# First projection of a fused two-block transformer kernel: six column groups for the first three pairs of x, four for the others, and attention six half-steps later

## What is computed

```python
mod = jax.nn.silu(c) @ w_ada[l] + b_ada[l]
sh_a, sc_a, gt_a, sh_f, sc_f, gt_f = [m[:, None, :] for m in jnp.split(mod, 6, axis=-1)]
h = rmsnorm(x, g_pre_attn[l]) * (1.0 + sc_a) + sh_a
proj = h @ w_in[l]
qa, ka, va, qb, kb, vb = jnp.split(proj, 6, axis=-1)
...
mix = jnp.concatenate([oa.reshape(B, S, WIDTH_A), ob.reshape(B, S, WIDTH_B)], axis=-1)
x = x + gt_a * rmsnorm(mix @ w_out[l], g_post_attn[l])
```

## Time and profile before

| | |
|---|---|
| median of 3 runs | 2367.99 us |
| profiled execution | 2367.4 us, its span 2365.6 us |
| TensorE (PE) busy | 2336.8 us, 99% of the span |
| VectorE (DVE) busy | 1816.1 us, 77% |
| ScalarE (ACT) busy | 1121.3 us, 47% |
| first projection, attention and output projection | 26 to 456 us of the span |
| TensorE idle in the span (span less busy) | 28.8 us |

### The profile page before, as it was taken

How to read it: one execution, slowest core, us unless ns; L and a number is a source line. 1 busy time by engine, 2 the same in 40 slices (tenths; PEclk the granted TensorE clock), 3 DMA queues, 4 the chain that set the end, 5 groups by cost and what they waited for, 6 DMA issues and landing times.

```text
span 2365.6 us, 26344 instructions
## 1 busy us (share of the span) xinstructions
PE 2336.8 (99%) x10358; PEld 1894.7 (80%) x10358; DVE 1816.1 (77%) x2447; ACT 1121.3 (47%) x1473; POOL 14.7 (1%) x31
## 2 busy tenths in 40 slices
PE   8999999999999999999999999999999999999998
PEld 5377788788888888888878888888888888888887
DVE  6788988888888888977565577997877795555775
ACT  5455676554444434444464334444345544444453
POOL 0000000000000000000000000000000000000000
PEclk9999999999999999999999999999999999999999
DMA  9987888887788777888746555556665556655553
GB/s 402 419 294 284 307 319 336 302 323 283 283 320 303 282 279 277 316 322 330 247 142 212 201 190 196 192 195 205 203 206 204 200 202 251 204 196 191 185 194 124
DMA packets 87758, 598.48 MB, mean 253 GB/s; under 512 B 10145, under 2 KB 10209, under 8 KB 16593
## 3 DMA queue, kind: packets, MB, share of 16 engines
q1 hardware_dynamic: 85538, 588.95, 69.2%
q0 software_dynamic: 1664, 7.19, 1.0%
q10 hardware_dynamic: 432, 0.66, 0.1%
HBM read 594.62 MB, written 2.13 MB: 252 GB/s over the span
## 4 chain that ended last, share of the span: by engine, by line
PE 91%; DVE 4%; DMA 3%; ACT 1%; issue 1%; DVEq 0%; ACTq 0%
PE PS L1181 20%; PE PS L1197 19%; PE PS L1198 19%; PE PS L1206 19%; PE PS L1186 10%; DMA RAW<-in_w_mod 2%; DVE RAW L1638 2%; DMA RAW<-in_w_first 1%; DVE LO L1628 1%; PE PS L1333 1%; PE PS L1552 0%; DVE X L1719 0%; PE PS L1270 0%; PE PS L1322 0%; ACT HI L669 0%
## 5 line engine op out<-in xcount | busy, mean ns | idle before, releaser
L669 ACT ACTIVATE HI<-RAW 128x1024 fp32r<-128x1024 f32 x784 | 828.4, 1059 | 1100.6 <-PE PS L1206 686.3
L1628 DVE TENSOR_TENSOR LO<-RAW,HI 128x1024 fp32r<-128x1024 f32 x784 | 956.7, 1223 | 461.9 <-ACT HI L669 457.9
L1197 PE MATMUL PS<-HI,XH 128*128 128x512 f32 x2080 | 821.8, 395 | 2.8 <-ACT HI L669 1.8
L1198 PE MATMUL PS<-HI,XL 128*128 128x512 f32 x2080 | 810.5, 390 | 0.0
L1206 PE MATMUL PS<-LO,XH 128*128 128x512 f32 x2080 | 558.3, 389 | 1.1 <-DVE LO L1628 1.1
L1197 PEld LDWEIGHTS PS<-HI,XH 128*128 128x128 f32 x2080 | 390.5, 188 | 87.4 <-DVE XL L1900 3.0
L1206 PEld LDWEIGHTS PS<-LO,XH 128*128 128x128 f32 x2080 | 390.2, 188 | 83.4 <-DVE LO L1628 1.6
L1198 PEld LDWEIGHTS PS<-HI,XL 128*128 128x128 f32 x2080 | 390.8, 188 | 78.9
L1181 PE MATMUL PS<-HI,XH 128*128 128x512 f32 x1056 | 325.9, 390 | 1.6 <-DVE XL L1742 1.1
L1181 PE MATMUL PS<-HI,XL 128*128 128x512 f32 x1056 | 325.2, 389 | 0.0
L1186 PE MATMUL PS<-LO,XH 128*128 128x512 f32 x1056 | 283.9, 389 | 0.0
(11 more groups left out here) (263 smaller groups left out, 891.6 us busy)
## 6 DMA issues: line engine op xcount, KB each, us to landing
RAW<-in_w_second SPq DMA_DIRECT2D x208, 1024.0 KB, 4.9
RAW<-in_w_mod SPq DMA_DIRECT2D x144, 1024.0 KB, 5.4
RAW<-in_w_ffn SPq DMA_DIRECT2D x88, 1024.0 KB, 4.9
RAW<-in_w_first SPq DMA_DIRECT2D x64, 1024.0 KB, 5.9
RAW<-in_w_down SPq DMA_DIRECT2D x44, 1024.0 KB, 5.1
BIAS<-in_b_in SPq DMA_DIRECT2D x40, 256.0 KB, 5.2
R<-mod_rows POOLq DMA_DIRECT2D x3, 1024.0 KB, 9.1
X<-in_x SPq DMA_DIRECT2D x2, 1024.0 KB, 8.7
```

Of the source, the lines that this page charges most:

```text
L669: act.activation(HI[:, (it["half"] + hf) % HLS, :], whole, ACT.Copy).then_inc(s.hi_ready, 1)
L1197: pe.matmul(PS[:, bank + u, :], XH[:, 2 * n + kk, rows], hi, start=start and kk == 0, stop=False)
L1198: pe.matmul(PS[:, bank + u, :], XL[:, 2 * n + kk, rows], hi, start=False, stop=False)
L1628: dve.tensor_tensor(LO[:, slot, :], RAW[:, it["slot"], hf * 1024:(hf + 1) * 1024], HI[:, slot, :].bitcast(F32), ALU.subtract).then_inc(s.l ...
```

## The change

Pairs 0 to 2 now serve six column groups: 4, 5, 2, 3 (halves 0 to 11, pair by pair), then 0 and 1 (halves 12 to 17). All 18 are direct. Groups 4 and 5 (v of the differential attention) begin in the PSUM banks of groups 0 and 1; ScalarE copies their partial sums to SBUF (`v_save`), groups 0 and 1 take the banks over, and the other five pairs of groups 4 and 5 run as halves 38 to 47. VectorE then adds the saved part (`v_add`). Pairs 3 to 7 serve groups 0 to 3 in halves 18 to 37, all in the split form. The A loads have a table of their own (`ADA_AHEAD`: how many A loads stand ahead of W load c), the later ones stand behind W loads 22 to 63 with two more behind 53 and 55. Rotations, turns, units and the first dilated heads stand six (dilated heads two, the norm and the turns of the first eight heads three or four) halves later; the 16 units now share 28 halves, so units 0 and 1 stand at 46 and 47, units 7 and 8 at 59 and 60, all others two apart.

```diff
-DIRECT = (0, 1, 2, 3)
-
-DIRECT_PAIRS = 6
-
-ADA_BEHIND = list(range(20, 64))
+AHEAD = 3
+
+PARTED = (4, 5)
+
+ADA_AHEAD = [4, 6, 8, 10, 12, 13, 14, 17, 19, 20, 22, 23, 24, 26, 28, 29, 29, 32]
+
+ADA_BEHIND = sorted([*range(22, 64), 53, 55])
...
-UNITS_AT = 40
+UNITS_AT = [46 + 28 * e // 15 for e in range(16)]
...
 def first_half(h):
 
-    if h < 8 * EARLY:
-        n, g = divmod(h, EARLY)
-    else:
-        g, n = divmod(h, 8)
+    if h < 4 * AHEAD:
+        n, r = divmod(h, 4)
+        g = (*PARTED, 2, 3)[r]
+        return g, n, n == 0, g in PARTED and n == AHEAD - 1
+    if h < 6 * AHEAD:
+        n, g = divmod(h - 4 * AHEAD, 2)
+        return g, n, n == 0, False
+    if h < 32 + 2 * AHEAD:
+        n, g = divmod(h - 2 * AHEAD, 4)
+        return g, n, False, n == 7
+    if h < 48:
+        g, n = divmod(h - 32 - 2 * AHEAD, 8 - AHEAD)
+        return PARTED[g], n + AHEAD, n == 0, n == 8 - AHEAD - 1
+    g, n = divmod(h, 8)
     return g, n, n == 0, n == 7
...
 def is_direct(h):
...
+    return h < 6 * AHEAD
...
-ROPE_AT = [31, 33, 35, 37, 59, 67, 75, 83]
-QK_TURN_AT = [(32, 33), (34, 35), (37, 38), (39, 40), (58, 60), (66, 68), (74, 76), (82, 84)]
+ROPE_AT = [37, 39, 41, 43, 59, 67, 75, 83]
+QK_TURN_AT = [(38, 39), (40, 41), (43, 44), (45, 46), (58, 60), (66, 68), (74, 76), (82, 84)]
...
-        if h - off == (74 + 2 * i if i < 4 else 76 + 2 * i):
+        if h - off == (76 + 2 * i if i < 4 else 78 + 2 * i):
...
+            def v_save(i):
+                g = PARTED[i]
+                act.wait_ge(s.half_used, 4 * AHEAD - 3 + i)
+                at = 1024 + 512 * i
+                act.activation(VO[:, :, at:at + 512], PS[:, first_bank(g):first_bank(g) + 2, :], ACT.Copy).then_inc(s.v_saved, 1)
...
-                if 92 <= h < 96:
-                    mtb_evac(h - 92)
+                if 95 <= h < 99:
+                    mtb_evac(h - 95)
...
-                if 88 <= h < 92:
-                    mixb_turn(h - 88)
+                if 91 <= h < 95:
+                    mixb_turn(h - 91)
...
+            def v_add(i):
+                g = PARTED[i]
+                dve.wait_ge(s.half_used, first_group_used(g))
+                dve.wait_ge(s.v_saved, i + 1)
+                v = VO[:, :, 1024 + 512 * i:1536 + 512 * i]
+                dve.tensor_tensor(v, PS[:, first_bank(g):first_bank(g) + 2, :], v, ALU.add).then_inc(s.v_added, 1)
...
+                if h == 46:
+                    v_add(0)
+                if h == 51:
+                    v_add(1)
```

More of the change, by code:

```diff
@@ L307, in first_body @@
 def first_body():
[L309 to L319, removed]
+    body = []
+    for c, n in enumerate(ADA_AHEAD):
+        body += [("A",)] * (n - body.count(("A",)))
+        body.append(("W", c))
+    for c in range(len(ADA_AHEAD), 64):
         body.append(("W", c))
@@ L904, in beside_first @@
                     qk_evac(*part)
-                if (i := v_at(h)) is not None:
+                if 4 * AHEAD <= h < 4 * AHEAD + 2:
+                    v_save(h - 4 * AHEAD)
+                if (i := v_at(h)) is not None and i >= 2:
                     v_evac(i)
@@ L958, in _ @@
                     hi_half(sec, 0, FIRST_W[0], 1)
-                if h < 8 * EARLY and h % EARLY == 0:
-                    x_pair(h // EARLY)
+                if (n := first_pair_at(h)) is not None:
+                    x_pair(n)
                 if 2 <= h < sec.n_halves:
@@ L1435, in _ @@
                     bank = first_bank(g)
-                    if start and g >= EARLY:
-                        before = g - 4 if g < 6 else g - 2
-                        if before in QK_GROUPS:
-                            pe.wait_ge(s.qk_out, QK_GROUPS.index(before) + 1)
-                        else:
-                            pe.wait_ge(s.v_out, V_GROUPS.index(before) + 1)
-                    if start and g == 5:
-                        pe.wait_ge(s.qt_ready, 6)
-                    if g == 0:
-                        pe.wait_ge(s.xh_ready if n < DIRECT_PAIRS else s.x_ready, n + 1)
-                    if h == 8 * EARLY:
-                        pe.wait_ge(s.x_ready, 8)
+                    if 4 * AHEAD <= h < 4 * AHEAD + 2:
+                        pe.wait_ge(s.v_saved, g + 1)
+                    if start and h >= 6 * AHEAD:
+                        held = g - 4 if g < 6 else g - 2
+                        if held in QK_GROUPS:
+                            pe.wait_ge(s.qk_out, QK_GROUPS.index(held) + 1)
+                        else:
+                            pe.wait_ge(s.v_added, V_GROUPS.index(held) + 1)
+                        if g == 5:
+                            pe.wait_ge(s.qt_ready, 4)
+                    if (pair := first_pair_at(h)) is not None:
+                        pe.wait_ge(s.xh_ready if is_direct(h) else s.x_ready, pair + 1)
                 else:
@@ L2100, in _ @@
                     h = it["half"] + hf
-                    if h < EARLY * DIRECT_PAIRS and h % EARLY == 0 and h:
-                        x_low(h // EARLY - 1)
-                    if h == EARLY * DIRECT_PAIRS:
-                        x_low(DIRECT_PAIRS - 1)
-                    if EARLY * DIRECT_PAIRS <= h < 8 * EARLY and h % EARLY == 0:
-                        x_low(h // EARLY)
+                    if h % 4 == 0 and 0 < h <= 4 * AHEAD:
+                        x_low(h // 4 - 1)
+                    if h >= 6 * AHEAD and (n := first_pair_at(h)) is not None:
+                        x_low(n)
                     if 96 <= h < 100:
@@ L2454, in first @@
     def first():
-        for n in range(16):
+        for n in range(48):
             yield [np.concatenate([rows(w["w_in"][:, W_IN_COLS[g]:W_IN_COLS[g] + 512], 2 * k, 2)
                                    for g, k, *_ in (first_half(2 * n), first_half(2 * n + 1))], axis=1)]
-        for n in range(16, 48):
-            g, k, _, _ = first_half(2 * n)
-            yield [rows(w["w_in"][:, W_IN_COLS[g]:W_IN_COLS[g] + 512], 2 * k, 4)]
         for g, k in W_OUT_CHUNKS:
```

55 lines of the change are left out of this document (29 added, 26 removed).

## The result

The changed kernel takes **2372.14 us**, the median of 13 executions (2368.28 to 2374.61); the kernel before took 2367.89 us on the same chip (13 executions). The ratio is 1.002, with a 95% interval of 1.0013 to 1.0028: slower by 0.2%. Forecast were 2364.0 us and a range from 2358 to 2370. The profiled execution took 2370.79 us, its span 2369.0 against 2365.6 us, so 3.4 of the 4.3 us between the medians are to be found in these two profiles.

The account below looks back on a forecast made before the run. TensorE, 99% busy, was taken as the bound, with loads setting the early pace. Terms 8.0 - 1.4 + 0.9 - 1.5 - 0.2 - 1.4 - 0.4 gave 4.0 us gain: profiled 2363.4, median 2364.0 us, range 2358 to 2370.

Parts of the forecast that it names:

- The start, +8.0: Up to pair 7: six more halves ahead of it, last reduction at 133.8, pair 7 at 139.5; gain 8.0 us.
- I take the second, so nothing is lost: Load buffers in the start: issue to landing takes 4.9 us as in the second block, not 7.6; cost nothing.
- The estimate of 4.4 us by the Trainium skill: Load time in the start: about 2.0 us plus bytes at 436 GB/s, by which the buffers suffice.
- `v_save`, costed at nothing: Two ScalarE copies of about 1 us, needed by TensorE three halves (10.7 us) later; cost nothing.
- The sine table was counted as a wait of VectorE, 1.8 us: Start: ScalarE's table load holds a load's second conversion back 1.8 us, most of VectorE's 2.6 us of waits.
- The rival in which the buffers run dry: Start: loads need 7.6 us from issue, pair 7 comes 8 us later, time about 2372; chance 0.08.
- The clock, -1.4: Behind the 4.0 us wait ahead of pair 7 TensorE runs at half speed; loss 1.4 us, 0 if idle comes in pieces.
- The first score and the later places, +0.9 - 1.5 - 0.2 - 1.4 - 0.4 = -2.6: Attention: lambda-table turn wait gone +0.9; unit 1's score -1.5; units 7 and 8 -0.2; half 74 turn -1.4; half 94 turn -0.4.
- The moved A loads, "meet a VectorE that is some 9 us ahead: nothing": Late in the section: two A loads moved behind W loads 53 and 55 meet VectorE some 9 us ahead; cost nothing.
- The announced signs: No TensorE waits 42 to 135 us; about 4 us near 139, then half speed; score waits 1 to 3, half 74 near 2.
- those named for a wrong forecast: Reductions waiting for loads 105 to 133 us, no second-score wait, TensorE waiting for VectorE at many units, halves waiting for `LO`.

Follow-up runs that it names:

- the tables alone: Changed kernel with only the sine and cosine tables moved from half 22 to half 19; 2369.61 us, ratio to the kernel before 1.0013.
- all three edits: Changed kernel with W load 4 one load later, both `v_save` behind the second conversion, tables at half 19 instead of 22; 2370.72 us, ratio 1.0007.
- e9_free_a_48_50: Changed kernel with all three edits, and the two later A loads behind W loads 48 and 50 instead of 53 and 55; 2366.63 us, ratio 0.9989.
- the run with zeros alone: Changed kernel with only four products of zeros added in TensorE's wait ahead of pair 7; 2371.20 us, ratio to the kernel before 1.0015.
- e12_a_48_50: Changed kernel with only the two later A loads behind W loads 48 and 50 instead of 53 and 55; 2369.59 us, ratio 1.0012.
- e1_start_free: Changed kernel with all three edits and nothing else; 2370.72 us, ratio to the kernel before 1.0007.
- e6_free_a_back: Changed kernel with all three edits, and the later A loads as before the change, one behind each W load from 20; 2367.72 us, ratio 1.0000.

## Why the prediction was wrong

**The start, +8.0: measured 4.3.** Part of the mechanism is as forecast: pair 7 follows the reductions of VectorE, back to back at the end, and the six halves ahead of it gain time. But the last reduction starts at 137.54, not at 133.8. The step that failed is the one on the buffers, "I take the second, so nothing is lost". Loads that were issued late took 6.7 to 7.8 us to land (loads 20, 24, 33, 38, 40), not the 4.9 of the second block; the lower bound was nearest to a stage with room, and this one is full. The estimate of 4.4 us by the Trainium skill (DMA: Bandwidth & Descriptors, Anatomy of one DMA) does not hold for these loads either: it rests on a fit for loads that GpSimd issues, and the shortest load of this section took 4.7 us. Two holders of a buffer were also missed: `x_pair(2)` ahead of the copies of W load 4, and `v_save`, costed at nothing because TensorE needs it late, though a load waits for the copy behind it. The sine table was counted as a wait of VectorE, 1.8 us, but as the holder of a buffer it was priced at nothing by the same 4.9. The runs with the tables alone and with all three edits show it: pair 7 moves with load 38, by 2.6 and 2.3 us. How much of this an execution keeps varies, as the profile of `e9_free_a_48_50` shows. The rival in which the buffers run dry had the right cause at the wrong size (8 us; 5.0 were lost). That its time, 2372, is what was measured is chance: the other half of that time comes from the end.

**The clock, -1.4: 1.3 by the run with zeros alone,** 1.6 with the slow first products of pair 7. Right for this profile; in the others without zeros the clock behind this wait cost 0.1 to 2.9 us. (The row of 42 to 44 us that the forecast reads lies ahead of 44.14; the window from 44 to 46 us has 1.00 as well.)

**The first score and the later places, +0.9 - 1.5 - 0.2 - 1.4 - 0.4 = -2.6: measured 2.8** from half 36 to half 97. The sum came out by chance; its parts did not. The turn's wait did not go (0.93 us at 181.52: its read-out stands behind a conversion whose load comes late), the second score waits 0.59 instead of 1.5, units 7 and 8 wait for nothing, turn and score behind the gate columns wait 1.16 us together against 0.54 before, and the turn at half 94 waits 0.66. Less the waits of the kernel before, these make 2.0 of the 2.8; the rest stands in no single wait.

**The moved A loads, "meet a VectorE that is some 9 us ahead: nothing": measured 5.7 us, of which 1.6 comes back.** In the sum of the two profiles this is the term that turned the sign; in the runs the change without it (`e12_a_48_50`) is still slower, by 0.12% instead of 0.20%, and only with the start mended too is it faster. The lead was there, 11.3 us at W load 53. But W loads 53 and 55 are now followed by two A loads each, three loads or 7.4 us for two halves of 5.4 us, and the lead falls to 7.0 us at W load 54 and 2.9 at 56. That is some 4 us each time, twice what this count gives: VectorE, whose reductions free the buffers, has more to do there as well. From 395 to 410 us it is busy 14.8 of 15 us (13.5 in the kernel before), and the share of the DMA engines is 0.93 to 1.00; which of the two sets the pace no run separates. From there to the end two halves take 5.4 us and their two loads 5.0, so the lead is hardly rebuilt (2.4 us at W load 62), and conversion and split of the last loads need more than that. I asked whether there was a lead and not what it must still cover. The run of the kernel before with this line alone (+4.3 us in the profile, 1.0031 in the runs) and that of the change with the two loads at 48 and 50 (-3.4 us) show it from both sides.

With the measured terms the sum is 4.3 - 1.6 - 2.8 - 5.7 + 1.6 + 0.7 = -3.5 us, against 3.4 us found. The announced signs came true in part: the wait ahead of pair 7 is there (3.2 us at 143 instead of 4 at 139), with the reductions ahead of it back to back and half speed behind it. But TensorE does wait between 42 and 135 us (2.75 us at 115.73). Of those named for a wrong forecast, a half that waits for `LO` came (1.77 us at 452.81). Reductions that wait for their loads between 105 and 133 us did not, although loads are late there: the conversions ahead of the splits wait for them.

## What to carry to other kernels

A load that the DMA engines work through without pause needs its buffer early: look for what stands between landing and the freeing instruction on each engine that must pass (another job's turn in the queue, a table load, an evacuation), and take the time from issue to landing from a stage that is equally full. A step that is moved into a stretch with a lead uses up that lead for everything up to the next point at which the lead is rebuilt; compare it with the least lead behind it, not with that at the place. Three small edits and a better place for two loads made the change faster than what it replaced, by 0.11% (0.02 to 0.20%, in one series).

## What the runs showed of the hardware that was not expected

The same wait costs different amounts of clock. Behind an idle time of 3.2 to 3.7 us ahead of pair 7, halves 34 and 35 took 7.04 us in the changed kernel, 8.38 and 8.32 in `e1_start_free` and `e9_free_a_48_50`, and 5.53 in `e6_free_a_back`, where the granted clock stayed at 2.4 GHz. Executions of one kernel lie 4 to 10 us apart here, those of the kernel before too (2365.6 to 2373.6 in one series of 27); the clock is part of that, how much was not measured. A profile of one execution therefore shows where a wait is, and only the series what it costs.

The time from issue to landing is not one number even in a full stage: load 30 of the changed kernel was issued at 84.08, landed at 89.39, 5.3 us later, and on time; load 38 took 6.7 us. The lead at issue does not settle it either: load 30 was issued 5.3 us ahead of its turn in all twelve profiles of the changed kernel and its variants, landed within 0.3 us of it in eleven and 2.1 us late in `e9_free_a_48_50`. Why, stays open.
